# An expert stage with its down biases taken ahead as rows of sums, and its last block apart

## The reference, cut to what matters

```python
logits = h @ w_router + b_router            # 32 experts
top_logit, top_idx = lax.top_k(logits, 4)
gate = softmax(top_logit)
# tokens sorted by expert, each expert's list padded to blocks of 128 slots
def expert_block(tok, g, e):
    gu = h_pad[tok] @ w_gate_up[e] + b_gate_up[e]
    y = clamped_swiglu(gu) @ w_down[e] + b_down[e]
    return y * g[:, None]
out = zeros.at[slot_tok].add(y)             # sum over a token's four experts
x = x + gt2 * out
return rmsnorm(x, g_final)
```

## Time and profile before

| what | value |
|---|---|
| median of three runs | 2475.66 us (2474.69 to 2476.12) |
| profiled execution | 2474.83 us, span 2473.0 us |
| granted TensorE clock, mean | 0.984 |
| expert stage with its end | from about 1250 us to 2473 us |
| blocks of 128 slots run | 32, 386 halves of weights |
| PE, DVE, ACT, POOL busy over the span | 97%, 82%, 53%, 28% |

### The profile page before, as it was taken

One profiled execution on the slowest core, in us unless ns is written; L12 is line 12 of the kernel. 1 busy time (PEld: TensorE's weight loads), 2 busy tenths in 40 slices (PEclk: granted clock), 3 DMA queues, 4 the chain that ended last, 5 costly groups with the idle time before them and its releaser, 6 DMA issues.

```text
span 2473.0 us, 31635 instructions
## 1 busy us (share of the span) xinstructions
PE 2400.4 (97%) x10905; PEld 1938.1 (78%) x10905; DVE 2020.5 (82%) x1839; ACT 1319.3 (53%) x1207; POOL 689.3 (28%) x409
## 2 busy tenths in 40 slices
PE   8999999999999999999969999999999999999995
PEld 7777788777877877887858888888888888888883
DVE  7787577576885796887379999999999999999994
ACT  4442223334423234425357777777777777777772
POOL 5343251333433423342322112211211221122120
PEclk9999999999999998999989999999999999999998
DMA  6232246221422672320099999999999999999992
GB/s 240 86 120 77 68 146 203 69 77 68 145 61 76 223 262 64 108 94 27 13 323 370 370 372 370 372 367 377 366 366 373 368 371 373 373 364 366 375 361 90
DMA packets 105989, 574.55 MB, mean 232 GB/s; under 512 B 15241, under 2 KB 15401, under 8 KB 55850
## 3 DMA queue, kind: packets, MB, share of 16 engines
q1 hardware_dynamic: 87770, 515.16, 55.7%
q0 software_dynamic: 17856, 58.25, 8.4%
q10 hardware_dynamic: 288, 0.14, 0.0%
HBM read 561.43 MB, written 26.22 MB: 238 GB/s over the span
## 4 chain that ended last, share of the span: by engine, by line
PE 87%; DVE 7%; DVEq 1%; DMA 1%; issue 1%; ACT 1%; POOL 1%; ACTq 0%; SPq 0%; POOLq 0%
PE ps L1585 84%; PE ps L1250 2%; DVE scr L2446 1%; DVE scr L2286 1%; DVEq L2448 1%; POOL pieces_split L2641 0%; DMA scr<-in_ada 0%; PE ps L695 0%; DVE mix L2337 0%; DVE y_split L2223 0%; DVE scr L2335 0%; DMA mix<-acc_rows 0%; DMA acc_rows<-rows,lst 0%; DVE w_split L1381 0%; DMA rows<-h_rows,slot_tokens 0%
## 5 line engine op out<-in xcount | busy, mean ns | idle before, releaser
L1381 DVE TENSOR_TENSOR w_split<-raw,w_split 128x2048 fp32r<-128x2048 f32 x386 | 877.7, 2288 | 52.9 <-ACT w_split L1332 41.8
L1585 PE MATMUL ps<-y_split,pieces_split 128*128 128x512 f32 x3600 | 846.3, 396 | 16.2 <-POOLq L2653 7.4
L1332 ACT ACTIVATE w_split<-raw 128x2048 fp32r<-128x2048 f32 x386 | 736.3, 1917 | 192.7 <-PE ps L1585 176.4
L1585 PEld LDWEIGHTS ps<-y_split,pieces_split 128*128 128x128 f32 x3600 | 680.4, 190 | 168.1 <-issue 26.3
L1585 PE MATMUL ps<-w_split,rows_T 128*128 128x512 f32 x3096 | 751.8, 394 | 0.1
L1585 PEld LDWEIGHTS ps<-w_split,rows_T 128*128 128x128 f32 x3096 | 575.2, 188 | 117.5 <-DVE rows_T L1387 0.6
L2641 POOL TENSOR_TENSOR pieces_split<-pieces,pieces_split 128x1024 fp32r<-128x1024 f32 x151 | 371.9, 2474 | 649.9 <-ACT pieces_split L1919 519.8
L1919 ACT ACTIVATE pieces_split<-pieces 128x1024 fp32r<-128x1024 f32 x144 | 151.3, 1058 | 426.9 <-PE ps L1585 395.9
L1585 PE MATMUL ps<-w_split,hidden_T 128*128 128x512 f32 x1536 | 363.5, 392 | 1.8 <-DVE hidden_T L1387 1.7
L1585 PEld LDWEIGHTS ps<-w_split,hidden_T 128*128 128x128 f32 x1536 | 285.9, 188 | 71.9 <-DVE hidden_T L1387 13.2
L1456 POOL COPY rows_i<-slot_tokens 128x1 int32 x32 | 56.6, 1768 | 370.0 <-PE ps L1250 369.5
(11 more groups left out here) (276 smaller groups left out, 2062.6 us busy)
## 6 DMA issues: line engine op xcount, KB each, us to landing
raw<-in_w_moe SPq DMA_DIRECT2D x386, 1024.0 KB, 7.4
pieces<-in_pieces SPq DMA_DIRECT2D x181, 512.0 KB, 3.5
scr<-in_ada POOLq DMA_DIRECT2D x48, 512.0 KB, 5.5
scr<-in_ple SPq DMA_DIRECT2D x2, 1536.0 KB, 7.1
acc_rows<-in_zeros POOLq DMA_DIRECT2D x5, 512.0 KB, 11.1
h_rows<-shift_row SPq DMA_DIRECT2D x1, 2052.0 KB
hT<-in_xT SPq DMA_DIRECT2D x8, 256.0 KB, 5.6
h_rows<-scr POOLq DMA_DIRECT2D x4, 512.0 KB, 7.7
```

What stands on the lines that cost most here:

```text
L1332: nc.scalar.activation(wsp[:, p % SPLIT, 0], raw[:, p % RAW, :], ACT.Copy).then_inc(high, 3 if p == 1 else 1)
L1381: nc.vector.tensor_tensor(wsp[:, p % SPLIT, 1], raw[:, p % RAW, :], wsp[:, p % SPLIT, 0].bitcast(F32), ALU.subtract).then_inc(low, 3 if p ...
L1585: return pe.matmul(out, lhsT, rhs, start=start, stop=stop)
```

## The change

*The down biases* are no longer added in the blocks. Before block 0, VectorE makes the gates by token and expert, TensorE turns them and multiplies them with the down biases in sixteen products (`z0` to `z7`). The results, for each token the sum of its gates times biases, are written to `acc_rows` instead of zeros, from buffers that the blocks use (`acc_begin`), so ScalarE, VectorE and GpSimd wait for `acc_init` ahead of the loop. The first down product of a block opens its sums.

*The last block* is written apart, as is the one before it; the loop runs one pair fewer. In the last one the two halves of a next expert, the fetch and the turning of rows are left out. Its rows are not scattered. SyncE loads `acc_rows` once block 30's rows are in, into two of the `raw` buffers. TensorE begins each of eight tiles with these sums by a product with the identity (`begun`), the first two of them ahead of its last two halves, and adds the last block's rows by a product with a one-hot of its tokens (`ended`). The sums of squares are taken by token with one-column products (`token_squares`), so that root and reciprocal are on four columns, and the inverse is spread by four products with diagonals.

```diff
+        accn = raw[:, 4:6, :].rearrange("p a b -> p (a b)").rearrange("p (t n) -> p t n", t=ST)
+        acc_begin = y_sb[:, 0, :], y_sb[:, 1, :], h_sb[:], act_buf[:, 0:2, :].rearrange("p a b -> p (a b)")
...
+            g = "gates"
+            pe.wait_ge(CV.free, CV.reusable(0, g))
+            pe.wait_ge(route_ready, GATES)
+            for t in range(ST):
+                m = pe.transpose(ps[0:2 * E_N, CV.bank(g), t * P:(t + 1) * P], gate_of[:, t].rearrange("p c e -> p (c e)"),
+                                 ident[:])
+            m.then_inc(CV.full, 1)
+            pe.wait_ge(bias_split, 1)
+            pe.wait_ge(route_ready, GATES_LOW)
+            for i in range(8):
+                g, t = f"z{i}", i // 2
+                pe.wait_ge(CA.free, CA.reusable(0, g))
+                out, at_ = ps[:, CA.bank(g), :], 2 * D + (i % 2) * S
+                mm(out, gate_T[0:2 * E_N, 0, t * P:(t + 1) * P], b_split[0:2 * E_N, at_:at_ + S], True, False)
+                mm(out, gate_T[0:E_N, 1, t * P:(t + 1) * P], b_split[0:E_N, at_:at_ + S], False, True).then_inc(CA.full, 1)
...
+            nc.vector.tensor_tensor(hot2, hot, value[:, :, 1:2].to_broadcast([P, ST * TOP, E_N]), ALU.mult)
+            dve.drain()
+            nc.vector.reduce_sum(gate_of[:, :, 0, :], hot2.rearrange("p (t k) e -> p t e k", k=TOP), AX.X)
+            dve.drain()
+            nc.vector.tensor_copy(gate_of[:, :, 1, :], gate_of[:, :, 0, :])
+            dve.drain().then_inc(route_ready, 1)
...
+            dve.wait_ge(gates_out, 1)
+            nc.vector.tensor_tensor(gate_T[0:E_N, 1, :], ps[0:E_N, CV.bank("gates"), :],
+                                    gate_T[0:E_N, 0, :].bitcast(F32), ALU.subtract).then_inc(route_ready, 1)
+            dve.drain().then_inc(CV.free, 1)
...
+                begins = j >= 4 and q == 0
...
                     for part in range(2):
-                        mm(ps[:, j, :], rows[:, part, at_:at_ + P], w[:, 0, k * S:(k + 1) * S], False, False)
+                        mm(ps[:, j, :], rows[:, part, at_:at_ + P], w[:, 0, k * S:(k + 1) * S], begins and k + part == 0, False)
...
+            def begun(k):
+                g = f"t{k}"
+                pe.wait_ge(DV.free, DV.reusable(0, g))
+                mm(ps[:, DV.bank(g), :], b_split[2 * E_N:P, 0:P], b_split[2 * E_N:P, 0:S], True, False)
+                for t in range(ST):
+                    mm(ps[:, DV.bank(g), t * P:(t + 1) * P], accn[:, t, k * P:(k + 1) * P], ident[:], False, False)
...
-                    pe.wait_ge(ye_ready, b + 1)
-                    bias(4, s)
-                    bias(5, s)
-                    pe.wait_ge(t_out, 3 * b + 4)
-                    run(6)
-                    run(7)
...
+                run(5)
+                pe.wait_ge(ye_ready, b + 1)
+                pe.wait_ge(t_out, turned + 1)
+                run(6)
+                run(7)
+                if not last:
                     pe.wait_ge(sel_ready, b + 2)
                     bias(0, 1 - s)
                     run(8)
-                    pe.wait_ge(act_ready, 2 * b + 4)
-                    turn(h_sb[:, S:D], 7).then_inc(t_full, 1)
+                pe.wait_ge(act_ready, 2 * b + 4)
+                turn(h_sb[:, S:D], 7).then_inc(t_full, 1)
+                if not last:
                     run(9)
-                    pe.wait_ge(t_out, 3 * b + 5)
-                    run(10)
-                    run(11)
-            final_pe(pe, mm)
+                else:
+                    pe.wait_ge(acc_in, 16 * ST)
+                    for k in range(2):
+                        begun(k)
+                pe.wait_ge(t_out, turned + 2)
+                run(10)
+                run(11)
+            with pe.Fori(0, n) as i:
+                for s in range(2):
+                    block_products(2 * i + s, i, s)
+            block_products(2 * n, n, 0)
+            block_products(2 * n + 1, n, 1, last=True)
+            final_pe(pe, mm, n, begun)
...
+            act.wait_ge(CV.full, CV.done(0, "gates"))
+            nc.scalar.activation(gate_T[0:2 * E_N, 0, :], ps[0:2 * E_N, CV.bank("gates"), :], ACT.Copy).then_inc(gates_out, 1)
+            high_part(1, 1, (raw_in[1], 16))
+            for i in range(8):
+                act.wait_ge(CA.full, CA.done(0, f"z{i}"))
+                nc.scalar.activation(acc_begin[i // 2][:, (i % 2) * S:(i % 2 + 1) * S], ps[:, CA.bank(f"z{i}"), :],
+                                     ACT.Copy).then_inc(CA.free, 1)
+                if i % 2:
+                    act.drain().then_inc(gates_out, 1)
             for q in range(2):
                 turned_high(xgT[:, 0, 0, q * S:(q + 1) * S], 6 + q, 1, q + 1)
+            act.wait_ge(acc_init, 16 * (ST + 1))
...
+            act.wait_ge(lst_ready, 2 * n + 3)
+            final_act(act, n)
...
+            dve.wait_ge(acc_init, 16 * (ST + 1))
...
+                        hidden_rows(b, 1)
+                    if p == 11 and last:
+                        dve.sem_inc(DV.free, 4)
+                        turned_low(hTe[:, 1, S:D], hTe[:, 0, S:D], 7, 1, turned + 2, 0.5)
+                        dve.drain()
+                        dve.sem_inc(DV.free, 2)
...
-            pool.wait_ge(acc_init, 16 * (ACC_ROWS // P))
             pool.wait_ge(list_ready, 1)
...
             take_list(0, 0)
+            for t in range(ST):
+                pool.wait_ge(gates_out, t + 2)
+                pool.dma_start(acc_dram[1 + t * P:1 + (t + 1) * P, :], acc_begin[t]).then_inc(acc_init, 16)
+            pool.wait_ge(acc_init, 16 * (ST + 1))
+            def block_rows(b, s, last=False):
+                pool.wait_ge(t_full, 3 * b + 2)
+                pool.sem_inc(pool_turns, 1)
+                if not last:
+                    fetch(b + 2, s)
+                add_rows(1 - s, b + 1)
+                pool.wait_ge(scattered, 16 * b + 16)
+                pool.sem_inc(pool_turns, 1)
+                if not (last and s):
+                    take_list(b + 1, 1 - s)
...
-            pool.wait_ge(scattered, 32 * n + 16)
+                    block_rows(2 * i + s, s)
             for s in range(2):
-                pool.wait_ge(xg_in[s], 16 * n + 16)
+                block_rows(2 * n + s, s, last=True)
             pool.sem_inc(z_ready, 1)
...
+        y_last = wsp[:, 2, :, 0:D]
+        token_at = wsp[:, 3, 0, 0:S]
...
-            sp.wait_ge(low, HALVES * 2 * n + FIRST + 2)
+            sp.wait_ge(low, half_at(2 * n + 1, 7) + 3)
...
+        def final_pe(pe, mm, n, begun):
+            def ended(k):
+                g = f"t{k}"
+                for part in range(2):
+                    m = mm(ps[:, DV.bank(g), :], y_last[:, part, k * P:(k + 1) * P], token_at, False, part == 1)
+                m.then_inc(DV.full, 1)
+            def token_squares(k):
+                pe.wait_ge(last_act, LAST_SQUARE(k))
+                for t in range(ST):
+                    m = mm(ps[:, 4, t:t + 1], xg_flat[:, k * S + t * P:k * S + (t + 1) * P], ones[:, 0:1], False,
+                           k == DK - 1 and t == ST - 1)
+                return m
...
+                if k % 4 == 0:
+                    pe.wait_ge(last_dve, k // 4 + 1)
+                ended(k)
+                if k == 4:
+                    mm(ps[:, 4, 0:ST], b_split[2 * E_N:P, 0:P], b_split[2 * E_N:P, 0:ST], True, False)
+                if k >= 5:
+                    token_squares(k - 5)
+                if k + 2 < DK:
+                    begun(k + 2)
+            for k in range(3, DK):
+                m = token_squares(k)
+            m.then_inc(last_pe, 1)
+            pe.wait_ge(last_dve, LAST_DIAG)
+            for t in range(ST):
+                m = mm(ps[:, 5, t * P:(t + 1) * P], ones[:], r_diag[:, t, :], True, True)
+            m.then_inc(last_pe, 1)
+        def final_act(act, n):
+            act.wait_ge(used, HALVES * 2 * n + 2 * HALVES + FIRST - 2)
+            for q in range(2):
+                nc.scalar.activation(y_last[:, 0, q * S:(q + 1) * S], ps[:, 4 + q, :], ACT.Copy,
+                                     scale=lst[:, 1, 1:2].bitcast(F32)).then_inc(last_act, 1)
...
+            dve.wait_ge(used, half_at(2 * n + 1, 7) + 1)
+            for t in range(ST):
+                nc.vector.tensor_scalar(token_at[:, t * P:(t + 1) * P], cst[:, 0:P], token_in[:, t:t + 1], None, ALU.is_equal)
+            for q in range(2):
+                dve.wait_ge(last_act, q + 1)
+                half_of = slice(q * S, (q + 1) * S)
+                nc.vector.scalar_tensor_tensor(y_last[:, 1, half_of], ps[:, 4 + q, :], lst[:, 1, 1:2].bitcast(F32),
+                                               y_last[:, 0, half_of].bitcast(F32), ALU.mult, ALU.subtract).then_inc(last_dve, 1)
...
             dve.wait_ge(std3_ready, 1)
-            nc.vector.reciprocal(glu, glu)
+            nc.vector.reciprocal(last_r, last_std)
             dve.drain()
+            for t in range(ST):
+                m = nc.vector.tensor_scalar(r_diag[:, t, :], ident[:], last_r[:, t:t + 1], None, ALU.mult)
```

(7 more changed lines are left out.)

224 lines of the change are left out of this document (112 added, 112 removed).

## The result

The changed kernel takes 2480.07 us, the median of 13 runs (2476.64 to 2482.88), against 2475.40 for the kernel before (13 runs, 2471.32 to 2477.44): a ratio of 1.0021 [1.0013, 1.0028], some 5 us slower. The forecast was 2474.3 and no measurable change.

What follows compares the result with a forecast made beforehand. The prediction took a loop through TensorE, ScalarE and VectorE, 36.09 us a block, as the bound. Blocks 0, end gain 11.4 and start loss 10.0 gave -1.4, so 2474.3 us on the median's scale, range 2460 to 2481.

Steps and rivals of the forecast that it cites:

- The blocks: Expert blocks: leaving out the down biases gains 0 (ends 0 and 14.0), since TensorE would wait 0.79 us for VectorE.
- TensorE's pace, the rival with 0.14: Expert blocks: TensorE sets the pace, so the dropped bias products gain 14.0 us, giving 2460.3; chance 0.14.
- The start: Before block 0: all engines wait for the first-row writes to land, at 1279.0 instead of 1269.0, losing 10.0 us.
- The hold of 5.71 us: Before block 0: GpSimd's second list copy stands still 5.71 us, delaying the writes queued behind it.
- The slower rival: Start: a second hold between the writes and weight loads sharing transfer engines delay the landing, giving 2482.5; chance 0.16.
- The last block: Last block: less work but a 2.0 us wait for the sums; last product at 2429.2 against 2431.6, gain 2.4.
- From the last product to the first output: Kernel end: 24.4 us from last product to first output operation, against 33.4 before.
- lower clock level in them: Sums of squares at the end: 1.5 us added for a lower granted clock in narrow products, ends 0 and 3.
- The sum: Whole kernel: blocks 0, end gain 11.4, start loss 10.0, together -1.4 us.
- the band of 0.2%: Whole kernel: differences within 0.2% (5 us, 2470.7 to 2480.6) count as no change.
- the likeliest case: Whole kernel: start and end sums of about 10 us cancel, nothing in the blocks; 2470.2 to 2479.7, chance 0.56.
- the rival on the good side: Start and end: writes land at 1276, no clock penalty, sums load sooner, up to 2469.3; chance 0.14.

Runs made afterwards that it cites:

- e1: Kernel before, with the two down-bias products left out of every block: 2476.29 us, ratio 1.0003.
- e3: Kernel before with only the last block and the end as in the changed kernel; zero rows and biases in blocks kept: 2468.09 us, ratio 0.9975.
- e12: Changed kernel with first rows in buffers not needed soon and weight loads from the fifth on held until the writes landed: 2474.59 us, ratio 0.9995.
- e7: Changed kernel with eight 512-column products for the sums of squares instead of 32 one-column ones, without diagonals: 2478.39 us, ratio 1.0015.
- e5: Changed kernel with weight loads from the fifth on held until the four first-row writes have landed: 2473.89 us, ratio 0.9995.
- e6: Changed kernel with first rows in buffers not needed soon, ScalarE's and VectorE's waits replaced by one at ScalarE's fourth conversion: 2473.48 us, ratio 0.9993.
- e4: Changed kernel with the first two tiles of sums begun behind the last block's last two halves, not ahead: 2477.22 us, ratio 1.0010.
- e8: Edits of e3 and e4 together, on the kernel before: 2464.18 us, ratio 0.9955.
- e11: e8 with tiles begun without a product of zeros and the wide sums of squares of e7: 2458.26 us, ratio 0.9930.
- e10: e8 with the wide sums of squares of e7: 2463.98 us, ratio 0.9951.

## Why the prediction was wrong

**The blocks (down biases worth 0): right.** The forecast let the wait grow to 0.79 in front of the last halves, 24 us in all. It came as two waits of some 0.46 a block, 28.5 to 31 us, and the period stayed. e1 and e3 exclude TensorE's pace, the rival with 0.14, which would have given 14 us.

**The start (loss of 10.0, ends 8.5 to 12.5): right in kind, 12.4 in size, and for other reasons.** Its step was that the "transposes, sixteen products and nine ScalarE evictions run while GpSimd is still held", so that the writes "are the late link, whatever TensorE and ScalarE do before". Both halves of it failed. The hold of 5.71 us was no fixed thing: it was 0.69 here and in e12, 0.78 in e7, 2.54 and 2.55 in e5 and e6, and 6.96 in e4. And GpSimd was not the late link in any of them: the last write waited for ScalarE's evictions, which follow TensorE's products, 1.68 us here and 2.35 even in e4, where the hold was longest. The products were counted only against GpSimd's queue. They also stand in TensorE's order ahead of the turning of block 0's rows, at the lower clock level (0.53 in the window from 1256 to 1268; in the 16 us before that TensorE was busy for 8.5); e6 and e12 leave 4.5 to 6.4 us of that with no wait for the landing at all. The landing was priced from four loads with nothing beside them, 8.7 from the first issue to the last landing, and from the old zero rows, 11.1; the chosen point left 8.6 from the last issue. It was 12.9, because the weight loads shared the engines; with nothing beside them each of these writes takes 2.9 to 4.0 (e5). That the size stayed inside its ends is in part luck: the last issue was 33.4 after MAX8 instead of the forecast's 35.3, set by the products and not by the hold, and the landing 12.9 instead of 8.6. The slower rival's mechanism had two halves. The hold did not come once more between the writes; the weight loads' share of the engines did come. Its last landing, from 1285.3 on, was not reached: 46.3 after MAX8 is 1281.4 on the clock of the kernel before.

**The last block (gain 2.4): right, 2.2.** Sums there 25.6 us after the block's start, as forecast; a wait of 1.76 for 2.0; last half at start + 34.1 for 34. One of its sums was off without effect: 2413.92 less the transposes (0.99) and the pair (0.45) is 2412.5 and not 2412.9, but TensorE then waited 0.66 for `hidden_T` and came 17.87 after the block's start, which is 2413.15. What the forecast missed is that the wait for the sums was not needed: with the tiles behind the halves nobody waits (e4, e8).

**From the last product to the first output (24.4): wrong, 28.4.** This is the term that decided. By its parts:

| part | forecast | measured |
|---|---|---|
| high and low part of the last rows | 1.5 | 1.6 |
| eight pairs of products | 3.6 | 4.4 |
| six tiles | 7.5 | 8.0 |
| sums of squares | 7.5 | 11.0 |
| lower clock level in them | 1.5 | in the 11.0 |
| root, inverse, diagonals, last four products | 2.8 | 3.5 |

The pairs were priced after the two biases in a block, 0.45; before a tile they take 0.67 (2441.62 to 2442.29), with the standing before its product of zeros. A tile takes 1.32 (to 2443.61) instead of 1.25. The 48 last one-column weight loads take 8.75 us, 0.182 each, where eight of them took 1.09 a little earlier: the granted clock was 1.00 from 2456 to 2458 and 0.50, the lower of the two levels, from 2460 on, although TensorE did not pause. The forecast had seen this after the routing's narrow products and allowed 1.5 for it; at the forecast's 0.117 each the 48 would take 5.6, so it was 3.1. The last four products then took 2.1 instead of 1.0 at that level. In other executions the same 48 took from 6.1 us (e8) to 9.0 (e6), so the 3.1 is this execution's. e7 and e11 show it from the other side: with wide products the clock stays up, and these take 5.31.

**The sum.** Start 2.4 more, end 4.2 less than forecast, together 6.6 on a sum of -1.4: +5.2. Neither alone would have left the band of 0.2%. The measured time lies inside the range of 2460 to 2481, just above the end of the likeliest case (2479.7). The chance of 0.16 for slower hung on one mechanism and was too small: two terms whose ends allowed 12.5 of loss and 8.5 of gain gave +4 by themselves. In the rival on the good side a landing at 1276 would be worth 3.0 and not 2.5.

**What stays open.** Why GpSimd's second list copy waits from 0.69 to 6.96 us was not tried; in the seven other kernels without first rows it waits 4.5 to 6.9, against 5.71 before. Nor was it tried why the products' clock and start differ between executions. The ends of matmuls in these rows are modelled, so parts of 0.1 us mean nothing. The table splits one execution.

## What to carry to other kernels

Work that is moved ahead of a loop is to be counted on every engine whose order it stands in, not only on the queue that looks latest: here TensorE's products cost as much as the landing. A write that many engines wait for should lie in buffers that are free for long, or go out while the big loads are held; one such line was worth 6 us. And what a removed instruction is worth is read from who waits next: products ahead of a wait are free (0 of 14 us), so the biases could have stayed where they were, and the end alone, with its tiles filling the hole behind the last halves, was worth 11 to 17 us.

## What the runs showed of the hardware

- Writes of 512 KB from on-chip memory landed in 2.9 to 4.3 us alone (e5, e12) and in 9.5 to 13.1 beside weight loads of 1 MB (changed kernel, e4, e6, e7).
- In a dense run of products with one column TensorE's granted clock fell from 1.00 (2456 to 2458) to 0.50 (2460 to 2465), while the matmul row was full (4.95 of the 5.00 us); products with 512 columns in the same place kept it at 1.00 (e7). The 48 one-column records took 6.1 to 9.0 us in nine profiles, the twelve wide ones 5.31 in each of three (e7, e10, e11).
- The product of zeros, with weights of 64 rows and 512 columns, took 0.43 us ahead of every tile (2442.29 to 2442.72), of it 0.24 to 0.25 of standing before the next weight load. The bias product with 128 rows and as many columns takes 0.225 (a pair in 0.45). Whether the number of rows or the change of it costs the difference was not tried.
